# A transformer layer in split fp32 matmuls: the inverse root of o's mean square as exp(-0.5 ln) on ScalarE, with its steps moved one interval

## The reference

```python
u = rmsnorm(x, norm_g[0]); proj = u @ w_in            # h, b, c, q, k, v and the gates
s = q_c k_c^T * HEAD_DIM**-0.5 - slope * |i - j|      # two maps c per head, 4 heads, 1024 x 1024
a = softmax(s1) - lam * softmax(s2)
o = a @ v                                             # 1024 x 128 per head
o = o * rsqrt(mean(o*o, -1) + 1e-6) * subln_g * (1 - lam_init)
m = (sigmoid(g0) * ((b * conv(c * h)) @ w_conv_out) + sigmoid(g1) * (o @ w_attn_out)) @ w_o
h = x + rmsnorm(m, g1)
out = h + rmsnorm(relu(rmsnorm(h, g2) @ w_ff1)**2 @ w_ff2, g3)
```

## Time and profile before

| | |
|---|---|
| median of 3 runs | 1378.68 us (1378.58 to 1378.86) |
| the profiled execution | 1378.79 us, its span 1377.1 us |
| PE busy | 1353.8 us, 98% of the span, 6305 matmuls |
| PEld (weight loads, beside PE) | 1108.9 us, 81% |
| DVE busy | 976.2 us, 71% |
| ACT busy | 641.6 us, 47% |
| POOL busy | 182.3 us, 13% |
| granted PE clock | 0.999 of full speed |
| DMA | 162.19 MB, 118 GB/s over the span |

### The profile page before, as it was taken

The page is one execution under the profiler, slowest core; times in us unless marked ns, Lnnn a source line. Parts: engine busy times, 40 slices in busy tenths (PEclk is TensorE's granted clock), DMA queues, the critical chain, the costliest instruction groups (busy, mean ns, idle before and its releaser), DMA issues.

```text
span 1377.1 us, 17129 instructions
## 1 busy us (share of the span) xinstructions
PE 1353.8 (98%) x6305; PEld 1108.9 (81%) x6305; DVE 976.2 (71%) x1456; ACT 641.6 (47%) x984; POOL 182.3 (13%) x103
## 2 busy tenths in 40 slices
PE   9999999999899999999999999999999999999998
PEld 8777777778688888888888888888888888888886
DVE  7687878888787644667466886767664786765676
ACT  7667777776332344511143453333333444444453
POOL 0232222220000000000000233333333100000000
PEclk9999999999999999999999999999999999999999
DMA  5110101012122232445721254444445973335342
GB/s 188 32 31 16 31 16 31 17 39 83 48 62 62 84 108 94 151 146 168 259 77 61 94 186 153 164 144 152 156 145 200 366 275 109 99 114 201 113 131 108
DMA packets 141657, 162.19 MB, mean 118 GB/s; under 512 B 6861, under 2 KB 88970, under 8 KB 141450
## 3 DMA queue, kind: packets, MB, share of 16 engines
q1 hardware_dynamic: 135568, 148.27, 33.4%
q10 hardware_dynamic: 6010, 12.88, 2.4%
HBM read 114.98 MB, written 46.14 MB: 117 GB/s over the span
## 4 chain that ended last, share of the span: by engine, by line
PE 72%; DVE 1%; issue 0%; DVEq 0%; ACT 0%
PE psum L1093 34%; PE psum L1253 22%; PE psum L929 13%; PE psum L1230 3%; PE psum L1202 1%; DVE v L2569 0%; DVE y L2584 0%; DVE norms L2558 0%; DVEq L299 0%; ACT y_junk L1615 0%; DVEq L2582 0%
## 5 line engine op out<-in xcount | busy, mean ns | idle before, releaser
L1253 PE MATMUL psum<-op 128*128 128x512 f32 x1344 | 305.1, 389 | 0.1
L1253 PEld LDWEIGHTS psum<-op 128*128 128x128 f32 x1344 | 252.2, 188 | 52.8 <-issue 0.5
L1716 ACT ACTIVATE op<-v 128x512 fp32r<-128x512 f32 x112 | 71.0, 634 | 149.2 <-PE psum L1253 145.3
L2448 DVE TENSOR_TENSOR op<-v,op 128x512 fp32r<-128x512 f32 x112 | 78.5, 701 | 86.8 <-ACT op L1716 86.8
L929 PE MATMUL psum<-act_hi,w_hi 128*128 128x512 f32 x256 | 103.2, 403 | 1.8 <-DVE act_lo L1855 1.1
L893 POOL TENSOR_TENSOR e<-e,e 128x1024 f32<-128x1024 f32 x31 | 74.6, 2407 | 228.2 <-ACT e L1382 228.2
L1375 ACT ACTIVATE e<-e,small 128x1024 f32<-128x1024 f32 x64 | 73.8, 1154 | 59.9 <-DVE small L1938 58.5
L1093 PE MATMUL psum<-act_hi,w_hi 128*128 128x512 f32 x256 | 99.8, 390 | 1.5 <-ACT prod L1464 0.8
L929 PE MATMUL psum<-act_hi,w_lo 128*128 128x512 f32 x256 | 100.2, 391 | 0.0
L929 PE MATMUL psum<-act_lo,w_hi 128*128 128x512 f32 x256 | 100.0, 390 | 0.0
L1093 PE MATMUL psum<-act_hi,w_lo 128*128 128x512 f32 x256 | 99.6, 389 | 0.0
(11 more groups left out here) (272 smaller groups left out, 3114.2 us busy)
## 6 DMA issues: line engine op xcount, KB each, us to landing
f_raw<-f_scratch SPq DMA_DIRECT2D x112, 256.0 KB, 2.7
w_raw<-in_w_ff SPq DMA_DIRECT2D x32, 512.0 KB, 5.4
w_raw<-in_w_in SPq DMA_DIRECT2D x28, 512.0 KB, 4.6
f_scratch<-f_out SPq DMA_DIRECT2D x56, 256.0 KB, 2.3
v<-in_w_ff SPq DMA_DIRECT2D x12, 1024.0 KB, 7.8
gates_scratch<-staging ACTq DMA_DIRECT2D x32, 256.0 KB, 2.0
gate_in<-gates_scratch SPq DMA_DIRECT2D x16, 512.0 KB, 4.3
f_scratch<-staging SPq DMA_DIRECT2D x30, 256.0 KB, 2.1
```

The costliest lines, as they stand in the source:

```text
L1253: mm = nc.tensor.matmul(psum[:, (X_BANK, Z_BANK)[m % 2][t]], op[n % SLOTS][:, 2 + a, token_cols(t)], op[n % SLOTS][:, b], start=(m in (0, ...
L1716: nc.scalar.activation(op[n % SLOTS][:, 0], v_block[m][:, kt], ACT.Copy).then_inc(v_hi, 1)
L2448: vec.tensor_tensor(slot[:, 1], v_block[m][:, kt], slot[:, 0].bitcast(F32), ALU.subtract).then_inc(v_split, 1)
```

## The change

- The square root on ACT and the reciprocal on DVE become `Ln` (reading the sums from PSUM, `o_logarithm`) and `Exp` with scale -0.5 in place (`o_inverse`), both on ACT; DVE's 32 reciprocals of 128 columns go.
- `o_sum` stands in the units of intervals 3 and 7 (before 4 and 0 of what follows), `o_logarithm` behind the exponentials of 3 and 7, `o_inverse` ahead of those of 4 and 0, `o_scale` in 1 and 5.
- `av_copy` is the first thing that DVE does in intervals 2 and 6; `o_squares` stands ahead of the exponentials there, `o_squares_lo` in the same interval.
- Behind the last head the order on ACT and DVE is another.

```diff
-O_IN = {filler(HEADS - 1, QB - 1): (HEADS - 1, 0)}
-for _i in range(1, HEADS):
-    O_IN[filler(_i, 0)] = (_i - 1, 0)
-    O_IN[filler(_i, 4)] = (_i - 1, 1)
+O_IN = {filler(_i, QB - 1): (_i, 0) for _i in range(HEADS)}
+O_IN.update({filler(_i, 3): (_i - 1, 1) for _i in range(1, HEADS)})
...
-            def o_deviation(i, n):
+            def o_logarithm(i, n):
                 act.wait_ge(o_done, half_at(i, n))
-                nc.scalar.activation(dev[:], o_bank(i, n), ACT.Sqrt, bias=eps,
+                nc.scalar.activation(dev[:], o_bank(i, n), ACT.Ln, bias=eps,
                                      scale=1.0 / (2 * HD)).then_inc(o_read, 1)
+
+            def o_inverse(i, n):
+                act.wait_ge(o_read, half_at(i, n))
+                nc.scalar.activation(dev[:], dev[:], ACT.Exp, scale=-0.5).then_inc(orstd_ready, 1)
...
-                    exponential(i, n, 1)
-                    exponential(i, n, 0)
                     if i > 0 and n in (0, 4):
-                        o_deviation(i - 1, n // 4)
-                    if n in (1, 3, 5):
-                        panel_hi(HEAD_PANELS * (i + 1) + n // 2)
-                    if i > 0 and n == 2:
+                        o_inverse(i - 1, n // 4)
+                    elif i > 0 and n == 2:
                         o_squares(i - 1, 1)
                     elif n == 6:
                         o_squares(i, 0)
+                    exponential(i, n, 1)
+                    exponential(i, n, 0)
+                    if i > 0 and n == 3:
+                        o_logarithm(i - 1, 1)
+                    elif n == 7:
+                        o_logarithm(i, 0)
+                    if n in (1, 3, 5):
+                        panel_hi(HEAD_PANELS * (i + 1) + n // 2)
...
             t_sum(GATE, 1, 0)
             turned_lo((last, "T", 7))
-            for part in range(4):
-                o_inverse(last, 0, part)
             o_scale(last, 0)
             t_sum(GATE, 1, 1)
             t_sum(GATE, 1, 2)
-            av_copy(last, 1)
+            t_sum(GATE, 2, 0)
             for x in ("W11", "W12"):
                 g_part_lo(x, p)
-            o_squares_lo(last, 1)
+            av_copy(last, 1)
             g_sum("S3", p)
             g_sum("S1", p)
+            o_squares_lo(last, 1)
             g_sum("S2", p)
-            t_sum(GATE, 2, 0)
             t_lo(GATE, 3)
+            t_sum(GATE, 2, 1)
             t_lo(GATE, 1)
-            t_sum(GATE, 2, 1)
             for x in ("S2", "S3", "S1"):
                 g_part_lo(x, p)
             t_sum(GATE, 4, 0)
             t_lo(GATE, 2)
+            t_sum(GATE, 4, 1)
             g_sum("S4", p)
             g_part_lo("W11", p + 1)
             g_part_lo("S4", p)
-            t_sum(GATE, 4, 1)
             t_lo(GATE, 4)
```

More of the change, by code:

```diff
@@ L918, in _, with product @@
         def _(pe):
-            def product(bank, stat, moving, kts, needs=(), between=None, at=None):
-                needs = dict(needs)
+            def product(bank, stat, moving, kts, needs=(), between=()):
+                needs, between = dict(needs), dict(between)
                 terms = [(kt, a, b) for kt in kts for a, b in PASSES]
                 for n, (kt, a, b) in enumerate(terms):
-                    if between and n == (at or len(terms) // 2):
-                        between()
+                    if n in between:
+                        between[n]()
                     if (a, b) == PASSES[0] and kt in needs:
@@ L1012, in scores, with unit @@
                 mm.then_inc(s_done, 1)
-            def unit(x, needs=(), between=None):
+            def unit(x, needs=(), between=()):
                 i, kind, n = x
@@ L1066, in _ @@
                     if (i, n) == (0, 0):
-                        unit(x, (), lambda: scores(0, 0))
+                        unit(x, (), {12: lambda: scores(0, 0)})
                         continue
@@ L2111, in head @@
                     maximum(i, n, 0)
-                    if n == 1 and i > 0:
-                        for part in (2, 3):
-                            o_inverse(i - 1, 0, part)
+                    if n in (1, 5) and i > 0:
+                        o_scale(i - 1, n // 4)
                     elif n == 2:
                         if i > 0:
-                            o_scale(i - 1, 0)
-                            av_copy(i - 1, 1)
+                            o_squares_lo(i - 1, 1)
                         panel_lo(HEAD_PANELS * (i + 1))
@@ L2141, in head @@
                     weights(i, n)
-                    if n in (0, 4) and i > 0:
-                        for part in range(2):
-                            o_inverse(i - 1, n // 4, part)
             for i in range(HEADS):
@@ L2230, in _ @@
                 if p == GATE.first + 2:
-                    for part in range(4):
-                        o_inverse(HEADS - 1, 1, part)
                     o_scale(HEADS - 1, 1)
```

48 lines of the change are left out of this document (21 added, 27 removed).

## The result

The change makes the kernel faster by 0.7%: a median of 1368.89 us (1368.68 to 1369.08, 6 runs) against 1378.78 (1378.58 to 1380.18, 6 runs of before beside it), ratio 0.9927, 95% interval 0.9915 to 0.9939. The prediction was 1369.2 us. The profiled execution took 1368.93 us, its span 1367.2; before it was 1378.79 and 1377.1.

A forecast was written before the change was run, and what follows sets the result against it. PE bounds the kernel, and only its idle time can move: +0.2 - 0.95 - 1.95 - 0.67 - 1.58 - 4.55 = -9.5 us, giving 1369.2 us against the median of 1378.68; range 1365.4 to 1374.2.

The forecast's parts named there:

- What bounds the kernel: PE, busy 1353.8 of 1377.1 us; the change can move only PE's idle time, 14.5 us of waits between 144 and 368.
- av in interval 5, heads 1 and 2: av's wait for the turned map: nothing gained, from 1.29 to about 1.4 us, twice 0.1, +0.2.
- Head 3: av's wait for the turned map in interval 5 of head 3 goes from 1.76 to 0.8 us, -0.95.
- av in interval 1: In heads 2 and 3 both waits of 0.97 us go, -1.95, with 0.35 to spare.
- The panel and o_sum: PE's wait for the panel's low part in head 3 goes, -0.67 us, and o_sum's for o's low squares, -1.58.
- The first pairs: Behind the last head, X1 to Z2: new wait of 1.0 us at X1, none at X2, X4, Y; -4.5 in all.
- X2's step: Sum 2's low part on DVE ends at 342.7, after losing 3.38 us of reciprocals and filling a 1.95 wait; X2 doesn't wait.
- Rival 1: The handover at the first pairs keeps its waits; only the heads' 3.4 and o_sum's 1.6 us stay: 1373.7; chance 0.16.
- Rival 4: Slower, a table switch costs more than 1.30 us: 13y less about 2.4 for y more per load, 1383.4 at y = 1.28; chance 0.03.
- the price of a switch: On ACT, a table load costs 1.28 us, 1.30 in all, without the Trainium skill's drain of about 1.38.
- Z2's own chain: Sum 4's low part begins at 352.5 and Z2 starts 8.7 us later at 361.2, before 367.34; Z2 waits 0.75.

The follow-up runs named there:

- e4: Changed kernel with o_sum of the second half earlier in interval 3's unit, logarithm and new exponential both ahead of the copy of the turned v: 1366.7 us.
- e5: Changed kernel with the edits of e3 and e4, but only logarithm and an Exp table load ahead of v's copy, new exponential in interval 4: 1364.29 us.
- e6: Changed kernel with one more table load (Sqrt's, used by nothing) ahead of each logarithm's, 8 loads more: 1376.27 us.
- e2: Kernel before with logarithm in the root's place, exponential ahead of the exponentials of intervals 5 and 1, no reciprocals, nothing moved: 1377.35 us.
- e7: Changed kernel with root and reciprocals back, but in the new order: 1368.52 us.
- e1: Changed kernel with ACT's and DVE's order behind the last head as before, without the reciprocals: 1374.52 us, profiled 1373.93.
- e3: Changed kernel with the last half's logarithm ahead of the high parts of sum 1 and of three weight blocks on ACT: 1367.52 us.

## Why the prediction was right, step by step

**What bounds the kernel** held: all that was gained is PE's idle time ahead of Z2, and the rest runs as it did (the earlier trace rows and its row after).

**av in interval 5, heads 1 and 2.** Right in kind, 0.15 to 0.2 off in size: the exponentials slip, and the wait is 0.40 + 0.80 where 1.4 was said (av starts 0.05 earlier, not 0.1 later). The text did not see that `scores` would stop too, for the maximum of the first map; it is the same delay, seen at two instructions. e4 and e5 show the chain as described (put the logarithm in ACT's idle time and the wait goes); e6 gives it a slope of one to one.

**Head 3**: 0.83 for the 0.8 that was said.

**av in interval 1.** The time was right and one reason was missing. The prediction took all of it from ACT (1.97 away, 0.65 back, 0.35 to spare). In e2, where ACT's 1.97 stay, the waits are 0.30 and 0.25 and not 0.97: two reciprocals ahead of DVE's low part were on this chain as well. With them the room is 0.35 + 0.67 = 1.0; e6 measured 0.7. The term was small by that, and nothing showed, since a wait that is gone can't shrink further.

**The panel and o_sum**: right. In e2 the missing reciprocals alone end both waits (o_sum's but for 0.26), and in e7 the new order alone ends both, so each of the two is enough.

**The first pairs.** The places were right: X1 waits 0.93 (said: 1.0), X2, X4 and Y not, X3 0.73, Z2 0.38 (0.75). What failed is one item in X2's step: "loses 3.38 us of reciprocals" was counted as time that DVE gains. By e1 and e2 it gains none: in e1 DVE stands 3.46 us ahead of `av_copy` instead, in e2 2.09 there and 1.3 more than before ahead of the last map's low part. It is the moved steps that fill this and the wait of 1.95; the sum came out, since 3.38 + 1.95 us of waits were indeed filled, though by another hand than the text says. So the prediction could not say what e7 shows, that the order without the swap is as fast. Rival 1, with 0.16, described e1: at 1373.7, for a measured 1373.9 in the profiled execution.

**Rival 4 and the price of a switch.** In all switches looked at here a load is 1.28 us and its neighbours follow within 0.02; e6 added eight for 7.4 us, of which seven were said to be on or near PE's path. The rule of the Trainium skill ("ScalarE: Activation LUTs", What ACT_TABLE_LOAD costs) of some 1.38 us of drain beside each would have made that some 17 us (7.7 + 7 x 1.38), an estimate from the page's figure; the trace does not agree. In the sum of rival 4 the "about 2.4" does not follow from the room that it names, 0.55 three times, which is 1.65; its times would be 0.75 higher.

**The 0.9 us that the sum lacked.** -9.5 was said up to Z2, -10.38 came. In the table 0.34 of it lies between X1 and Z2, 0.26 at o_sum, and the rest in pieces of 0.15 and less. The 0.34 is Z2's own chain, whose sum was 0.37 too long: sum 4's low part begins 14.63 us behind X1 (348.23 and 333.60), where 352.5 - 337.5 = 15.0 was said, and its 8.7 to Z2 are right (8.73). So Z2 waits 0.38 for the 0.75 that was said. The 0.26 is the price of a stop. A stop of PE between two matmuls of 512 columns costs more than the idle time in brackets. X3, after:

```profile
344.33 0.39 PE L1093 MATMUL psum<-g_t_hi,g_S_lo 128*128 128x512 f32 x1
345.45 0.47 PE L1093 MATMUL psum<-act_hi,g_S_hi 128*128 128x512 f32 x1 [0.73 <-issue]
345.76 0.39 PE L1093 MATMUL psum<-act_lo,g_S_hi 128*128 128x512 f32 x1
```

From 344.33 to 345.76 are 1.43 us for two matmuls that take 0.45 at the pitch of 0.227: the stop costs 0.97, and 0.73 is shown. The prediction took o_sum's wait at its bracketed 1.58, and 1.84 came; e3 got 1.17 for X1's 0.93. Behind `scores` a stop costs hardly more than it shows (0.97 was shown in interval 1, 1.03 came), and from X1 to Z2 the prediction went by distances between starts, which have the price in them. Half of the 0.9 was hidden again by the longer last transfer, which the prediction did not have: that 1369.2 met 1368.89 so closely is in part luck.

Not settled: why the last transfer of `out` takes 0.5 us more, and what decides whether PE's clock falls behind a wait like e6's 2.22 us.

## What to carry to other kernels

Ask of a removed operation what its engine will do in its place: if the next instruction in its order waits for another engine, nothing is gained until work is moved there. An engine without idle time ahead of an instruction may still have been exactly on time for a wait. Move an operation to where its own engine waits for something outside the chain (ACT's 2.87 us for PE's turning of v), not to where it waits for the answer to its own last result. And count the stops of the bounding engine as well as their idle time.
